# A streaming encoder step with a sparse attention and 32 experts: gate and up products in split precision, and an expert's weights loaded by one transfer

## The reference

```python
h = rms_norm(x, norm_mix_g)
z_pool, q, k, v, qi, ki, wi, ga, gb = jnp.split(h @ w_in, SPLIT_POINTS, axis=-1)
...
def hier_moe(h, w_rg, b_rg, w_re, b_re, w_g, w_u, w_d):
    g_logits = h @ w_rg + b_rg                      # 4 groups, one is taken
    e_logits = (h @ w_re + b_re)[that group]        # 8 experts in it, two are taken
    comb = softmax weights of the two, times the group's probability, 0 elsewhere
    act = silu(h @ w_g[e]) * (h @ w_u[e])           # 1024 -> 128, for each expert e
    out = sum over e of (act * comb[e]) @ w_d[e]    # 128 -> 1024
```

## Time and profile before

| | |
|---|---|
| three runs | 1378.94, 1371.85, 1379.20 us, median 1378.94 |
| profiled execution | 1371.11 us, span 1368.7 us, mean granted clock 0.982 |
| busy share of the span | PE 95%, PEld 82%, DVE 61%, POOL 35%, ACT 30% |
| DMA over the span | 163.78 MB, mean 120 GB/s |
| in the chain that ended last | PE 88% (line 1159: 8%, line 1165: 4%) |

### The profile page before, as it was taken

One profiled execution on the slowest core, in us unless ns is written; L12 is line 12 of the kernel. 1 busy time (PEld: TensorE's weight loads), 2 busy tenths in 40 slices (PEclk: granted clock), 3 DMA queues, 4 the chain that ended last, 5 costly groups with the idle time before them and its releaser, 6 DMA issues.

```text
span 1368.7 us, 21310 instructions
## 1 busy us (share of the span) xinstructions
PE 1302.6 (95%) x7759; PEld 1118.9 (82%) x7759; DVE 830.4 (61%) x2070; ACT 416.3 (30%) x938; POOL 474.1 (35%) x772
## 2 busy tenths in 40 slices
PE   5999999999989999997999999999999989999986
PEld 5978999999979999996666656999788758888852
DVE  5454778888999999836677656243565622222226
ACT  5554222122221122226555444100332212121213
POOL 4800595868882127541000010220011233233314
PEclk9999999999999999999999999999999989999997
DMA  7201232122223222002000220734201058999847
GB/s 252 71 24 43 69 91 79 38 75 39 68 61 110 77 84 62 2 1 97 1 17 1 65 83 15 299 139 177 108 32 47 33 217 313 390 331 344 317 197 320
DMA packets 71118, 163.78 MB, mean 120 GB/s; under 512 B 12529, under 2 KB 38721, under 8 KB 69873
## 3 DMA queue, kind: packets, MB, share of 16 engines
q1 hardware_dynamic: 56929, 129.31, 27.0%
q0 software_dynamic: 12656, 27.62, 6.0%
q10 hardware_dynamic: 1440, 5.58, 1.0%
HBM read 137.81 MB, written 39.21 MB: 129 GB/s over the span
## 4 chain that ended last, share of the span: by engine, by line
PE 88%; POOL 3%; DVE 3%; ACT 3%; DMA 1%; issue 1%; ACTq 0%; POOLq 0%; SPq 0%; DVEq 0%
PE bank L790 11%; PE bank L791 11%; PE bank L792 11%; PE bank L1159 8%; PE bank L988 5%; PE bank L1165 4%; PE bank L1059 3%; PE bank L1053 3%; PE bank L975 3%; PE bank L912 2%; PE bank L1071 2%; PE bank L1070 2%; PE bank L1072 2%; PE bank L1152 2%; PE bank L1013 2%; PE bank L1055 2%
## 5 line engine op out<-in xcount | busy, mean ns | idle before, releaser
L1651 DVE MAX8 small<-region_kv 128x8 f32<-128x272 f32 (+4 forms) x241 | 190.2, 828 | 51.3 <-DVE region_kv L1656 51.2
L790 PE MATMUL bank<-h_hi,w_hi 128*128 128x384 f32 (+1 forms) x576 | 196.1, 340 | 0.0
L791 PE MATMUL bank<-h_lo,w_hi 128*128 128x384 f32 (+1 forms) x576 | 196.1, 340 | 0.0
L1656 DVE MATCH_REPLACE8 region_kv<-small,region_kv 128x272 f32<-128x272 f32 (+4 forms) x241 | 195.5, 818 | 0.0
L792 PE MATMUL bank<-h_hi,w_lo 128*128 128x384 f32 (+1 forms) x576 | 194.4, 338 | 0.0
L1950 POOL TENSOR_TENSOR w_lo<-w_stage,w_hi 128x512 fp32r<-128x512 f32 x64 | 80.8, 1296 | 149.6 <-ACT w_hi L1243 149.5
L790 PE MATMUL bank<-w_hi,h_hi 128*128 128x256 f32 x448 | 129.9, 290 | 1.4 <-ACT region_q L1303 1.4
L792 PE MATMUL bank<-w_hi,h_lo 128*128 128x256 f32 x448 | 125.9, 281 | 0.0
L791 PE MATMUL bank<-w_lo,h_hi 128*128 128x256 f32 x448 | 125.9, 281 | 0.0
L792 PEld LDWEIGHTS bank<-h_hi,w_lo 128*128 128x128 f32 x576 | 108.7, 189 | 0.0
L791 PEld LDWEIGHTS bank<-h_lo,w_hi 128*128 128x128 f32 x576 | 108.2, 188 | 0.6
(11 more groups left out here) (282 smaller groups left out, 2893.1 us busy)
## 6 DMA issues: line engine op xcount, KB each, us to landing
w_stage<-in_w_in SPq DMA_DIRECT2D x72, 256.0 KB, 3.1
region_kv<-in_xa SPq DMA_DIRECT2D x16, 512.0 KB, 5.3
region_q<-in_wg SPq DMA_DIRECT2D x12, 512.0 KB, 8.7
region_q<-in_wu SPq DMA_DIRECT2D x12, 512.0 KB, 21.2
region_q<-in_wd SPq DMA_DIRECT2D x12, 512.0 KB, 22.9
region_h<-in_wg SPq DMA_DIRECT2D x12, 512.0 KB, 11.3
region_h<-in_wu SPq DMA_DIRECT2D x12, 512.0 KB, 20.3
region_h<-in_wd SPq DMA_DIRECT2D x12, 512.0 KB, 23.5
```

The source lines that it names most:

```text
L790: mm(out, st_hi(k), mv_hi(k), start=(k == 0), stop=False)
L791: mm(out, st_hi(k), mv_lo(k), start=False, stop=False)
L1651: nc.vector.max(m8[:, q, :], x).then_inc(dve_c, 1)
L1656: nc.vector.match_replace(x, m8[:, q, :], x, TAKEN).then_inc(dve_c, 1)
```

## The change

- **Gate and up** become three fp32r products in split precision. The rows are now the stationary operand and gate and up side by side the moving one, 256 columns: 24 products (`gate_up_split`). For that ScalarE rounds an expert's gate and up, two casts of 1024 columns, two experts ahead (`expert_upper`), and VectorE subtracts (`expert_lower`), in place in the slot; the transposed rows are split in the same manner (`rows_upper`, `rows_lower`). The result has tokens on partitions, so the activations are multiplied there and then turned by one more transpose on TensorE (`turn_act`) and one copy on ScalarE.
- **Order.** The down product of e-1 now follows gate and up of e and the transposes of e+1. The two halves of the output rows are scaled by VectorE (`first_half`) and ScalarE (`second_half`).
- **Gathers and scatters.** GpSimd's loop issues the gather of e+3, then the scatter of e-1.
- **Weights.** Gate, up and down of an expert lie side by side in HBM, and `load_e` is one transfer of 128 lines of 12 KB. There are seven slots in place of eight.
- **Start.** The indexer's eight steps have eight stage buffers, four of them new, and all eight are loaded ahead of the third tile of tokens. ScalarE's and VectorE's lists are changed to match: the third and fourth tile are squared and scaled behind the eight casts and subtractions.

Much of the diff is buffers, and the same waits under other names; its core:

```diff
@@
-                 + [RH[:, 3072 * i:3072 * i + 3072] for i in range(3)])
+                 + [RH[:, 3072 * i:3072 * i + 3072] for i in range(2)])
...
             load_x(0)
             load_x(1)
-            for m in range(2):
+            for m in range(KD):
                 load_step(0, m)
-            load_x(2)
-            for m in range(2, 4):
-                load_step(0, m)
-            load_x(3)
-            load_x(4)
-            for m in range(4, KD):
-                load_step(0, m)
+            for tt in range(2, 5):
+                load_x(tt)
...
             def load_e(e):
                 s = e % NSLOT
-                sp.dma_start(eslot[s][:, 0:1024], a["wg"][e]).then_inc(ew_in[s], 16)
-                sp.dma_start(eslot[s][:, 1024:2048], a["wu"][e]).then_inc(ew_in[s], 16)
-                sp.dma_start(e_down(s), a["wd"][e]).then_inc(ew_in[s], 16)
+                sp.dma_start(eslot[s], a["we"][e]).then_inc(ew_in[s], 16)
...
+            def gate_up_split(e):
+
+                par = e % 2
+                out = bank[6 + par][:, 0:2 * P]
+                rest, high = e_rest[e % NSLOT], e_high[par]
+                pe.wait_ge(wao_high, 3 * KD + 2 * e + 2)
+                pe.wait_ge(wao_low, 3 * KD + 2 * e + 2)
+                pe.wait_ge(te_evac, 2 * e + 2)
+                if e >= 2:
+                    pe.wait_ge(act_ready, e - 1)
+                for k in range(KD):
+                    mm(out, rowsT_hi[:, par, k, :], high[:, :, k, :], start=(k == 0), stop=False, skip_group_check=True)
+                    mm(out, rowsT_hi[:, par, k, :], rest[:, :, k, :], start=False, stop=False, skip_group_check=True)
+                pe.wait_ge(rows_low, 2 * e + 2)
+                for k in range(KD):
+                    last = mm(out, rowsT_lo[:, par, k, :], high[:, :, k, :], start=False, stop=(k == KD - 1),
+                              skip_group_check=True)
+                last.then_inc(gu_done, 1)
+
+            def turn_act(e):
+                pe.wait_ge(act_ready, e + 1)
+                nc.tensor.transpose(bank[6 + e % 2][:, 2 * P:3 * P], act_rows[:, e % 2, :], ident).then_inc(act_turned, 1)
+
+            def down_of(e):
+                pe.wait_ge(actT_ready, e + 1)
+                if e >= 2:
+                    pe.wait_ge(y_ready, e - 1)
+                    pe.wait_ge(y_act, e - 1)
+                down(e % NSLOT, e % 2)
...
             for e in range(NE):
-                pe.wait_ge(ew_in[e % NSLOT], 48 * (e // NSLOT + 1))
-                pe.wait_ge(te_evac, 2 * e + 2)
-                if e >= 2:
-                    pe.wait_ge(act_ready, e - 1)
-                gate_up(e, e % NSLOT, e % 2)
+                gate_up_split(e)
                 if e + 1 < NE:
                     e_trans(e + 1)
-                pe.wait_ge(act_ready, e + 1)
-                if e >= 2:
-                    pe.wait_ge(y_ready, e - 1)
-                down(e % NSLOT, e % 2)
+                if e >= 1:
+                    down_of(e - 1)
+                turn_act(e)
+            down_of(NE - 1)
...
+            def expert_upper(e):
+                act.wait_ge(ew_in[e % NSLOT], 16 * (e // NSLOT + 1))
+                if e >= 2:
+                    act.wait_ge(gu_done, e - 1)
+                cp(e_high[e % 2][:, 0, :, :], e_gate(e % NSLOT)).then_inc(wao_high, 1)
+                cp(e_high[e % 2][:, 1, :, :], e_up(e % NSLOT)).then_inc(wao_high, 1)
...
+            expert_upper(0)
+            expert_upper(1)
+            rows_upper(0)
             for e in range(NE):
...
+                act.wait_ge(gu_done, e + 1)
+                if e >= 2:
+                    act.wait_ge(act_ready, e - 1)
+                silu_e(e % 2)
+                if e + 1 < NE:
+                    rows_upper(e + 1)
+                if e + 2 < NE:
+                    expert_upper(e + 2)
+                act.wait_ge(act_turned, e + 1)
+                if e >= 2:
+                    act.wait_ge(dn_done, e - 1)
+                cp(actT[:, e % 2, :], bank[6 + e % 2][:, 2 * P:3 * P]).then_inc(actT_ready, 1)
+                if e >= 1:
+                    second_half(e - 1)
+            second_half(NE - 1)
...
-            for e in range(NE):
+            for e in range(NE + 1):
                 if e + 3 < NE:
                     pool.wait_ge(te_done, 2 * (e + 1))
                     gather(hg[:, e % 3, :], gidx[:, e + 3:e + 4], hg_in[e % 3])
-                pool.wait_ge(y_ready, e + 1)
-                scatter(ysb[:, e % 3, :], heads[:, e, 0:1], y_out[e % 3])
+                if e >= 1:
+                    y = e - 1
+                    pool.wait_ge(y_ready, y + 1)
+                    pool.wait_ge(y_act, y + 1)
+                    scatter(ysb[:, y % 3, :], heads[:, y, 0:1], y_out[y % 3])
```

More of the change, by code:

```diff
@@ L94, in build @@
             w_out_hi = out_weights_hi.enter_context(nc.sbuf_tensor("w_out_hi", [P, KD, D], F32R))
+        e_rest = [None] * 7
+        with ExitStack() as slots_q:
+            for q in range(2, 5):
+                e_rest[q] = slots_q.enter_context(nc.sbuf_tensor(f"expert_rest{q}", [P, 2, KD, P], F32R))
+                slots_q.enter_context(nc.sbuf_tensor(f"down_of_slot{q}", [P, D], F32))
         RQ = sb("region_q", [P, 9216])
@@ L1614, in _ @@
             h_rows(1)
-            split_lo(0, 0, 4)
-            for i in range(10):
+            split_lo(0, 0, 2)
+            h_rest(0)
+            split_lo(0, 2, 6)
+            h_rest(1)
+            split_lo(0, 6, 8)
+            h_rows(2)
+            h_rows(3)
+            for i in range(2, 10):
                 h_rest(i)
@@ new lines, in _ @@
+            expert_lower(0)
+            expert_lower(1)
+            rows_lower(0)
+            for e in range(NE):
+                dve.wait_ge(silu_done, e + 1)
+                if e >= 2:
+                    dve.wait_ge(act_turned, e - 1)
+                tt(act_rows[:, e % 2, :], silu[:, e % 2, :], bank[6 + e % 2][:, P:2 * P], ALU.mult).then_inc(act_ready, 1)
+                if e + 1 < NE:
+                    rows_lower(e + 1)
+                if e >= 1:
+                    first_half(e - 1)
+                if e + 2 < NE:
+                    expert_lower(e + 2)
@@ L1893, in _ @@
+            first_half(NE - 1)
             dve.wait_ge(over_in, 32)
```

138 lines of the change are left out of this document (89 added, 49 removed).

## The result

| | before | after |
|---|---|---|
| median of runs, us | 1375.4 (4 runs, 1371.3 to 1379.2) | 1388.1 (4 runs, 1386.6 to 1388.6) |
| ratio, 95% interval | | 1.0102 [1.0076, 1.0127] |
| profiled execution, us (span) | 1371.1 (1368.7) | 1386.6 (1384.9) |
| mean granted clock of TensorE | 0.982 | 0.975 |

The change makes the kernel 1.0% slower. 1373 us was forecast, 5.7 us less than the median of the three runs before; the four runs of each kernel above give 12.7 us more. The measured median lies within the outer range (1354 to 1392) only because that took in half of rival C's price; the forecast's own case ended at 1378. "Slower by over 0.5%" had a chance of 0.23.

The account below looks back on a forecast made before the run. Expert stage taken as bound by TensorE and, just behind it, the busier half of the DMA engines. TensorE's part -4.7, output rows -0.6, start -0.4: -5.7 us, from 1378.9 to 1373 us; range 1354 to 1392.

Parts of the forecast that it names:

- rival C: Expert stage: gathers starve behind 12 KB lines, landing up to 15.4 us; 1407 us, at half price 1392; chance 0.19.
- own case: Expert stage: busier half of DMA engines sets pace, 6.24 us per expert; 1373 us, range 1366 to 1378; chance 0.48.
- Gathers and scatters: Expert stage: gathers issued 6.4 us after gate and up leave 12.3 us for a landing of 8.6; no cost.
- What bounds the kernel now: Expert stage bound twice: by TensorE, 6.24 us per expert, and just behind by the busier half of DMA engines, 6.51.
- The rate of long lines: Weight loads: 12 KB lines move 434 GB/s, 217 for the busier half, taking its share from 6.51 to 6.24 us.
- Gate and up: Expert stage: cheaper products cut TensorE's share to 5.63 us per expert, 0.61 less; alone 19.5 us.
- The split: Expert stage: ScalarE 4.3 and VectorE 4.8 us per expert, beside TensorE's 5.63, costed at nothing.
- Overflow table and seven slots: Weight loads restart behind the table 6.5 us earlier, at 1147.2, by terms of 3.9, 1.3 and 1.3 us.
- The start: Kernel start: transposes behind the third tile's rows begin at 18.8, not 19.19; -0.4 us, bounds -2 and +1.
- Low clock: Expert stage: the low clock might return in TensorE's pauses of some 0.6 us per expert; no cost given.
- B: Expert stage: no relief, long lines bring nothing and 6.51 us per expert stays; 1381 us; chance 0.16.
- A: Expert stage: TensorE keeps the bound, DMA engines below 5.63 us per expert; 19.5 us less, 1358 us; chance 0.17.

Follow-up runs that it names:

- e9: Kernel after, still one transfer per expert but with lines of 4 KB in place of 12 KB: 1375.2 us.
- e3: Kernel after, with each expert's list laid over the partitions so that its rows fall on all 16 DMA engines: 1375.3 us.
- e11: Kernel after, with three transfers of 4 KB lines per expert and rows over all DMA engines, overflow table read back where the change has it: 1356.8 us.
- e1: Kernel after, with each expert loaded by three transfers of 4 KB lines: 1372.9 us.
- e8: Kernel before, with rows over all DMA engines and the overflow table read back later: 1372.5 us.
- e7: Kernel after, with three transfers of 4 KB lines per expert, rows over all DMA engines and the overflow table read back later: 1352.4 us.
- e5: Kernel after, with the overflow table read back after seven more experts are loaded: 1387.9 us.

## Why the prediction was wrong

**The step that failed** is "Gathers and scatters": "At 6.24 that leaves 12.3 us for a landing of 8.6: nothing, as long as it stays below 12." The condition was right; the landing was taken from lines of 4 KB and left there, although the change triples the line. Measured: 12.4 us in the median and up to 23.0, and TensorE's weight loads wait 29.5 us for rows. Rival C had the mechanism and the point, 12.3 us, from which it costs. That its half price, 1392, is near the measured 1388 is luck: by its own formula the median would give (6.4 + 12.4)/3 = 6.27 us for an expert, next to no loss. Most of the loss is in what one landing for all doesn't show. From the down product at 1151.12 to that at 1201.25, six experts take 8.36 us each, 12.7 us more than at 6.24: the gathers of up to 23 us, the next ones that go out late behind them, and the low clock. The fourteen experts from there to 1293.06 take 6.56 each, 4.5 us more. What C was denied in the text, that late gathers throttle the loads that delay them, did not save it. With three lines' worth in each turn the loads finish early (0.2 us of waits for weights) and only the rows are late.

**Two figures of the text were read as independent that are one.** Weights late and rows in time (4 KB), or weights early and rows late (12 KB): the earlier trace rows gives the first division and the changed line the second. I priced the line's effect on the weights (6.51 to 6.24 us) and let the rows be. (The Trainium skill, "DMA: Bandwidth & Descriptors", section on queues and rings, says that an engine changes queues only at packets; by e9, where only the line differs, that rule and this trace agree, and 10.9 KB for each packet is what the text had no row for.)

**What bounds the kernel now**: right. That the rows load the DMA engines unevenly is shown by the spread alone, with the same bytes: e3 (22.8 us less of stage) and, with 4 KB lines, e11 against e1 (19.7). TensorE's bound just beside them is shown by e8 (next to nothing gained).

**Own case, 6.24 us for an expert by the busier half**: not reached with long lines, since rows bound first. With short lines (e1) the forecast's figure for them, 6.51, gives 1151.1 (restart) + 25 x 6.51 + 11.9 = 1325.8 for the end of TensorE's part; measured 1322.0.

**The rate of long lines**: too high. 434 GB/s was forecast by a straight line through 4 and 8 KB, 217 for the busier half. From 1119 to 1135 us, nearly all loads, the kernel after moves

```profile
DMA packets 952, 6.73 MB, mean 421 GB/s; under 512 B 266, under 2 KB 266, under 8 KB 473
```

where 404 was the figure for 4 KB: somewhat over half of the gain. It decided nothing, since the rows bound.

**Gate and up**: right. TensorE's share was forecast at 5.63, measured 5.57 (e7). Its full worth was put at 19.5 us, and e8 less e7 is 20.1 (with the rest of the change in it).

**The split**: ScalarE and VectorE stay within TensorE's share: in e7 they are busy 36.0 and 41.2 of 50 us, that is 4.0 and 4.6 us for each expert, where 4.3 and 4.8 were forecast.

**Overflow table and seven slots**: loads restart at 1144.5, not 1147.2: 9.2 us earlier than before, where 6.5 was forecast. Which of its three terms was too small, no run shows. It decided nothing (e5).

**The start**: -0.4 forecast. The third tile's transposes start at 18.45 instead of 19.19, but the gathers begin at 1111.9 where they began at 1111.0: nothing is left of it.

**Low clock**: named as a danger in the last paragraph and priced by no row. It came: granted 0.86 from 1150 to 1200 us, with transposes of 1.97 and down products of 3.47 us. An estimate from these rows: 0.87 us more for the transposes twice, and 1.6 for the down product three times, make 6.5 of the stage's 13.5 us more. It was not tried apart.

**B and A**: A's time (1358) would have needed rows that don't wait; e7, with short lines and the rows spread, is below it. B's loss of relief was not what bound.

## What to carry to other kernels

When a transfer's lines are made longer, price the other queue, not the lengthened one: the bytes are the same, but here a gather that shares the DMA engines with it landed after 12.4 us instead of 9.0 in the median, and after 23.0 instead of 10.4 at worst, and a chain that had just enough lead broke. Look for the step with the least slack against its landing before looking at the mean rate. And if a stretch of half-used DMA engines shows up, ask which partitions the small transfers touch: spreading 72 rows over all 128 partitions was worth 20 to 23 us of stage after the change and 2 before it, where TensorE had no wait to lose.

## What was not expected of the hardware

- A load of 1.5 MB in 12 KB lines lands in 9.8 us beside the gathers, the same load in 4 KB lines in 27.5 (e9), at much the same total rate (323 GB/s in 1150 to 1310 after the change, 337 in e9).
- GpSimd is held longer by a scatter beside VectorE's subtractions of the weights. Its scatters took 1.01 us each before, and after:

```profile
L2266 POOL DMA_INDIRECT expert_rows_scratch<-region_t,small_i x32 | 46.8, 1461 | 129.5 <-ACT region_t L1621 125.2
```

1.46 us in the mean, and 2.07 where one stands beside 2.35 us of subtractions (POOL at 1166.87, VectorE's two L1983 at 1165.71). By the starts and lengths in the two engines' timelines, 1123 to 1307 us, all 26 scatters overlap a subtraction, and each takes 0.88 us and the overlap: 1.16 with 0.28, 1.48 with 0.59, 2.07 with 1.19. In e1 the same subtractions fall elsewhere: 24 of 27 scatters overlap none and take 1.00 to 1.02 us, the other three 1.15 to 1.48. A gather is not held: one that overlaps a subtraction by 0.53 us takes 1.01 (e1, e7). In e7, with TensorE never waiting, the longer scatters cost nothing. The Trainium skill, page "Advanced Engine Details and Errata", section "GPSIMD Details", says that GpSimd shares a read and a write interface with VectorE and conflicts with those of its instructions that run in a two-port mode or have two inputs in SBUF. The subtraction of the weights has two such inputs; for the scatters the trace agrees, for the gathers it shows no conflict.
